# Routing on the unnormalised residual in a two-layer decoder trunk, with the residual's rows turned one tile pair at a time

## The reference

```python
x = x + y @ w_o[l]
h = rms_norm(x, ffn_norm[l])          # x / sqrt(mean(x*x) + eps) * gain
# layer 0: x = x + swiglu(h, wg, wu, wd)
# layer 1:
logits = (h @ router)                 # 256 x 8
topv, topi = top_k(logits, 2)
gates = softmax(topv)
# every expert e computes swiglu(rows of h that chose e) and adds gate * result to those rows of x
```

## Time and profile before

| | us |
|---|---|
| three runs | 1672.48, 1673.81, 1678.3; median 1673.81 |
| the profiled execution, its own time | 1672.51 |
| its span in the trace | 1670.7 |
| layer 0: mixers, dense part (to the last down product) | 0 to 467 |
| layer 1: mixers (to the last output product) | 476 to 671 |
| layer 1: norm and routing, to the first expert matmul | 671 to 702.5 |
| eight experts | 702.5 to 1661 |
| busy: TensorE, VectorE, ScalarE, GpSimd | 97%, 73%, 62%, 4% |

### The profile page before, as it was taken

How to read it: one execution, slowest core, us unless ns; L and a number is a source line. 1 busy time by engine, 2 the same in 40 slices (tenths; PEclk the granted TensorE clock), 3 DMA queues, 4 the chain that set the end, 5 groups by cost and what they waited for, 6 DMA issues and landing times.

```text
span 1670.7 us, 28450 instructions
## 1 busy us (share of the span) xinstructions
PE 1614.5 (97%) x10924; PEld 1397.2 (84%) x10924; DVE 1212.5 (73%) x1378; ACT 1034.5 (62%) x1286; POOL 60.5 (4%) x70
## 2 busy tenths in 40 slices
PE   7998989999999999799999999999999999999997
PEld 6887889999987878788888888888888888888885
DVE  1365454545424654489999999999999999999996
ACT  2334344444423343378888888888887887888885
POOL 0004000000000040000000000000000000000000
PEclk9999989999989999799999999999999999999999
DMA  6502165555414202599999999999999999999994
GB/s 202 179 17 104 55 224 178 186 192 177 159 56 152 101 4 75 183 355 376 341 392 393 352 394 394 349 395 390 350 395 388 356 393 373 366 395 362 386 385 144
DMA packets 192359, 445.59 MB, mean 267 GB/s; under 512 B 9088, under 2 KB 11664, under 8 KB 192144
## 3 DMA queue, kind: packets, MB, share of 16 engines
q1 hardware_dynamic: 187040, 433.49, 70.8%
q0 software_dynamic: 2160, 7.87, 2.1%
q10 hardware_dynamic: 3072, 3.01, 0.5%
HBM read 438.04 MB, written 6.29 MB: 266 GB/s over the span
## 4 chain that ended last, share of the span: by engine, by line
PE 95%; DVE 2%; ACT 1%; issue 1%; DMA 0%; POOL 0%; SPq 0%; ACTq 0%; DVEq 0%; POOLq 0%
PE bank L692 24%; PE bank L694 24%; PE bank L693 24%; PE bank L675 16%; PE bank L788 3%; PE bank L1234 1%; PE bank L700 1%; DMA arena<-in_consts 0%; ACT acts_hi L1297 0%; PE bank L1037 0%; DVE acts_lo L2066 0%; PE bank L1173 0%; PE bank L795 0%; DVE w_lo L1828 0%; DVE w_lo L1837 0%
## 5 line engine op out<-in xcount | busy, mean ns | idle before, releaser
L1297 ACT ACTIVATE w_hi<-ring 128x1024 fp32r<-128x1024 f32 x772 | 815.4, 1060 | 293.2 <-PE bank L694 292.5
L1837 DVE TENSOR_TENSOR w_lo<-ring,w_hi 128x1024 fp32r<-128x1024 f32 x672 | 813.0, 1224 | 67.5 <-ACT w_hi L1297 19.6
L692 PE MATMUL bank<-w_hi,acts_hi 128*128 128x512 f32 x1344 | 528.4, 393 | 7.1 <-DVE acts_lo L2066 5.7
L694 PE MATMUL bank<-w_hi,acts_lo 128*128 128x512 f32 x1344 | 523.7, 390 | 0.0
L693 PE MATMUL bank<-w_lo,acts_hi 128*128 128x512 f32 x1344 | 523.4, 389 | 0.0
L692 PEld LDWEIGHTS bank<-w_hi,acts_hi 128*128 128x128 f32 x1344 | 252.4, 188 | 59.9 <-issue 5.9
L694 PEld LDWEIGHTS bank<-w_hi,acts_lo 128*128 128x128 f32 x1344 | 252.2, 188 | 53.0
L693 PEld LDWEIGHTS bank<-w_lo,acts_hi 128*128 128x128 f32 x1344 | 252.5, 188 | 50.9
L1828 DVE TENSOR_TENSOR w_lo<-ring,w_hi 128x1024 fp32r<-128x1024 f32 x84 | 102.7, 1225 | 118.8 <-ACT w_hi L1297 118.8
L692 PE MATMUL bank<-acts_hi,w_hi 128*128 128x256 f32 x608 | 174.8, 287 | 1.6 <-DVE acts_lo L1646 1.6
L693 PE MATMUL bank<-acts_lo,w_hi 128*128 128x256 f32 x608 | 173.5, 285 | 0.0
(11 more groups left out here) (202 smaller groups left out, 1216.8 us busy)
## 6 DMA issues: line engine op xcount, KB each, us to landing
ring<-in_moe_wg SPq DMA_DIRECT2D x112, 1024.0 KB, 7.0
ring<-in_moe_wu SPq DMA_DIRECT2D x112, 1024.0 KB, 7.2
ring<-in_moe_wd SPq DMA_DIRECT2D x112, 1024.0 KB, 7.0
ring<-in_w_in SPq DMA_DIRECT2D x24, 1024.0 KB, 6.4
ring<-in_dense_wg SPq DMA_DIRECT2D x14, 1024.0 KB, 5.2
ring<-in_dense_wu SPq DMA_DIRECT2D x14, 1024.0 KB, 5.1
ring<-in_dense_wd SPq DMA_DIRECT2D x14, 1024.0 KB, 4.8
ring<-in_w_o SPq DMA_DIRECT2D x8, 1024.0 KB, 7.4
```

The lines of the kernel that those rows point to most:

```text
L692: pe.matmul(out_, a_hi, b_hi, start=first, stop=False, **kw)
L694: return pe.matmul(out_, a_lo, b_hi, start=False, stop=final, **kw)
L1297: return act.activation(o, i, ACT.Copy, **kw)
L1837: TT(w_lo[:, q, :], raw, w_hi[:, q, :].bitcast(F32), ALU.subtract).then_inc(lo_ready, 1)
```

## The change

- **Splits one pair earlier, both layers.** Pieces 0 and 1 of block g are split after pair 0 and pieces 2 and 3 after pair 1, on ScalarE and VectorE.
- **Router on the residual.** At the start of layer 1 VectorE multiplies `router_w` by the norm's gain (`router_set`). `turn_rows(i)` on TensorE turns pair i of `xT` as soon as it is added and multiplies `xT` with the router weights: nothing for pair 0, tiles 0 to 3 with pair 1, then two tiles each with pairs 2 and 3. In layer 1 `spread_rms`, the 8 scalings of `hT` and the turning of `hT` are gone. The square sums, root and reciprocal stay; the reciprocal scales the difference of the two best logits and, later, the rows.
- **Rows.** ScalarE keeps the turned `xT` (`keep_rows`), half 0 before the root and half 1 after it. VectorE makes `h_tok` as `x_tok` * reciprocal * gain in two halves (`normal_rows`), the gain read from a new input of 128 equal rows (512 KB, one DMA on ScalarE's queue, issued once the mixers are done).
- **First one-hot alone.** VectorE makes expert 0's one-hot (`hot_first`, 256 columns) straight from the counts; the ranks come after it, and the one-hot of all experts, the gates and the token numbers after the split of the gathered rows (`place_tokens`).
- **Writes of the rows.** `h_rows` and `out` are written by ScalarE's queue after the split of the gathered rows.
- `x_tok` and `h_tok` lie elsewhere, so that they can be written while the mixers' tensors are in use.

```diff
@@ -1045,6 +1053,23 @@
+            def turn_rows(i):
+                pe.wait_ge(wo_added, 4 * (L - 1) + i + 1)
+                for k in (2 * i, 2 * i + 1):
+                    for b in range(2):
+                        last = pe.transpose(bank[ROWS_BANKS[k // 4][b]][:, k % 4 * P:(k % 4 + 1) * P],
+                                            xT[:, k, b * P:(b + 1) * P], ident)
+                if i % 2:
+                    last.then_inc(pe_turned, 1)
+                pe.wait_ge(router_set, 1)
+                for k in ((), range(4), (4, 5), (6, 7))[i]:
+                    for b in range(2):
+                        last = pe.matmul(bank[1][:, b * NE:(b + 1) * NE], xT[:, k, b * P:(b + 1) * P], router_w[:, k, :],
+                                         start=k == b == 0, stop=k == KT - 1, skip_group_check=True)
+                if i == 3:
+                    last.then_inc(logit_done, 1)
@@ -1110,10 +1135,14 @@
                     if j:
                         sum_squares(2 * l + 1, 2 * j - 2)
                         sum_squares(2 * l + 1, 2 * j - 1)
+                        if l:
+                            turn_rows(j - 1)
+                if l:
+                    turn_rows(3)
                 sum_squares(2 * l + 1, KT - 2)
                 sum_squares(2 * l + 1, KT - 1)
-                spread_rms(2 * l + 1)
                 if l == 0:
+                    spread_rms(1)
@@ -1157,30 +1186,13 @@
-            for b in range(2):
-                for k in range(KT):
...
-            for f in range(8):
...
-                last.then_inc(pe_turned, 1)
@@ -1264,9 +1278,10 @@
-                pe.wait_ge(oh_ready, p + 1)
-                if p == 0:
-                    pe.wait_ge(act_turned, 4)
+                if p:
+                    pe.wait_ge(oh_ready, p + 1)
+                else:
+                    pe.wait_ge(hot_ready, 1)
                 gather(0, first)
@@ -1319,14 +1334,22 @@ (ScalarE)
-                    if between and i in (1, 2):
-                        between(range(2 * i - 2, 2 * i))
+                    if between and i < 2:
+                        between(range(2 * i, 2 * i + 2))
+                if then_keep:
+                    then_keep()
@@ -1940,15 +1968,15 @@ (VectorE)
-                    if j in (1, 2):
-                        pieces = range(2 * j - 2, 2 * j)
+                    if j < 2:
+                        pieces = range(2 * j, 2 * j + 2)
@@ -2010,17 +2038,34 @@ (VectorE)
             TT(sel, first, second, ALU.add).then_inc(route_sel, 1)
-            TT(e2, top2, top1, ALU.subtract).then_inc(route_act, 1)
+            then(TT(e2, top2, top1, ALU.subtract))
+            dve.wait_ge(rt_ready, 4)
+            then(dve.reciprocal(rms, rms))
+            TT(e2, e2, rms, ALU.mult).then_inc(route_act, 1)
+
+            def normal_rows(hf):
+                dve.wait_ge(act_turned, 2 * hf + 2)
+                hs = slice(hf * CW, (hf + 1) * CW)
+                for b in range(2):
+                    last = STT(h_tok[:, b, hs], x_tok[:, b, hs], rms[:, b:b + 1], gain_rows[:, hs], ALU.mult, ALU.mult)
+                last.then_inc(ht_ready, 1)
+
+            dve.wait_ge(gain_in, 16)
+            normal_rows(0)
             dve.wait_ge(rank_done, 1)
+            then(STT(rank_first, per(bank[6][:, 0:16])[:, :, 0], 1.0, per(sel)[:, :, 0], ALU.add, ALU.mult))
+            STT(hot_first, spread(const("iota"), 2), 1.0, stretch(rank_first, P), ALU.add,
+                ALU.is_equal).then_inc(hot_ready, 1)
+            normal_rows(1)
@@ -2090,9 +2134,14 @@ (VectorE, place_tokens is the old head of moe_pass)
                 first = p * NE
-                gathered(first)
                 if p:
+                    then(TS(rank, rank, -float(P), None, ALU.add))
+                    place_tokens()
+                    gathered(first)
                     split("g", 0, first)
+                else:
+                    gathered(first)
+                    place_tokens()
                 split("u", 0, first)
```

More of the change, by code:

```diff
@@ L120, in decoder_trunk @@
 def decoder_trunk(nc, x, consts, masks, params, lora, vres_v2, w_in, vres_w, w_o, dense_wg, dense_wu, dense_wd,
-                  router, moe_wg, moe_wu, moe_wd, h_rows, out):
+                  router, gains, moe_wg, moe_wu, moe_wd, h_rows, out):
     with ExitStack() as ctx:
@@ L235, in decoder_trunk @@
         sil_b = [moe.take(CW) for _ in range(2)]
+        hot_first = moe.take(2 * P).rearrange("p (b s) -> p b s", b=2)
+        moe.take(max(0, 22 * T - moe.at))
+        x_tok = moe.take(2 * D).rearrange("p (b d) -> p b d", b=2)
+        h_tok = moe.take(2 * D).rearrange("p (b d) -> p b d", b=2)
+        gain_rows = spare[:, 0:D]
         dense = Region(arena[:, phase:ARENA], ARENA - phase)
@@ L1157, in _ @@
                     norm(2)
-            for b in range(2):
-                for k in range(KT):
[L1162 to L1166, removed]
-            for f in range(8):
[L1169 to L1174, removed]
-                last.then_inc(pe_turned, 1)
             sel = small[:, 0:16]
             pe.wait_ge(route_sel, 1)
[L1179 to L1183, removed]
+            mm(bank[6][:, 0:8], const("tri"), sel[:, 0:8])
+            mm(bank[6][:, 8:16], const("tri"), sel[:, 8:16], True, False)
+            mm(bank[6][:, 8:16], ones, sel[:, 0:8], False, True)
+            mm(bank[6][:, 16:24], ones, sel[:, 0:8], True, False)
+            mm(bank[6][:, 16:24], ones, sel[:, 8:16], False, True).then_inc(rank_done, 1)
             def moe_pass(p):
@@ L1320, in split_in, with keep_rows, norm @@
                     copy(w_hi[:, q, :], ring[:, slot_of[n], q % 2 * PIECE:(q % 2 + 1) * PIECE]).then_inc(hi_ready, 1)
-            def norm(n, ready, between=None):
+            def keep_rows(hf):
+                act.wait_ge(pe_turned, hf + 1)
+                for b in range(2):
+                    copy(x_tok[:, b, 512 * hf:512 * (hf + 1)], bank[ROWS_BANKS[hf][b]][:, :]).then_inc(act_turned, 1)
+            def norm(n, ready, between=None, then_keep=None):
                 done, base, tiles = ready
@@ L1513, in _ @@
                 recurrence(l)
-                norm(2 * l + 1, (wo_added, 4 * l, 2), lambda pieces: split("g", 0, 0, pieces) if l else dense_split("g", 0, pieces))
+                if l:
+                    act.wait_ge(y_out, L)
+                    act.dma_start(gain_rows, gains).then_inc(gain_in, 16)
+                norm(2 * l + 1, (wo_added, 4 * l, 2), lambda pieces: split("g", 0, 0, pieces) if l else dense_split("g", 0, pieces),
+                     (lambda: keep_rows(0)) if l else None)
                 if l == 0:
@@ L1847, in _ @@
                     h_low_part(2 * l, k)
+                if l:
+                    gain0 = N_PARAM * l + PARAM_COLS["ffn_norm"][0]
+                    TT(router_w, router_w, stretch(prm[:, gain0:gain0 + KT], NE), ALU.mult).then_inc(router_set, 1)
                 head_factor(2 * l, 4, 1.0 / HD, NORM_EPS, (ALU.mult, ALU.add))
@@ L1949, in _ @@
                 dve.wait_ge(wo_added, 4 * l + 4)
-                norm(2 * l + 1, l, "ffn_norm")
                 if l == 0:
+                    norm(1, 0, "ffn_norm")
                     def dense_multiply(j):
@@ L1999, in _ @@
             dve.wait_ge(logit_done, 1)
-            then(TS(logits, bank[0][:, 0:16], 1.0, None, ALU.mult))
+            then(TS(logits, bank[1][:, 0:16], 1.0, None, ALU.mult))
             def largest(value, hot):
```

66 lines of the change are left out of this document (34 added, 32 removed).

## The result

The changed kernel takes 1658.07 us (median of 4 runs, 1657.62 to 1660.04) against 1673.19 for the kernel before: ratio 0.9915, 95% interval 0.9898 to 0.9933, 15.1 us less. Timed a second time, beside the two kernels of experiment 9, it came to 1660.31 us and 0.9927 (0.9913 to 0.9941). Forecast: 1659.7. The profiled execution took 1657.62, its span 1655.8, 14.9 less than before.

The account below looks back on a forecast made before the run. TensorE was taken as the bound, at 95% of the span. Layer 0's 1.7 us plus 12.4 before the first expert matmul made 14.1 off 1672.51, 1658.4, or 1659.7 on the median's footing; range 1655 to 1667.

Parts of the forecast that it names:

- The bound: Whole kernel: TensorE is 95% of the span, so an earlier first expert matmul moves the end by as much.
- Layer 0, 1.7: Layer 0's norm: splits one pair earlier bring the first dense matmul 1.7 us forward.
- the late sums: Layer 0's norm: TensorE's sums for the pair before stand in front of the last ones, losing 0.2 us.
- TensorE's order in layer 1: Layer 1's routing: transposes and router matmuls between the products; logits done at 676.7 and no longer at 685.4.
- Selection: Layer 1, logits to gathering: counts at low clock 2.2 us, costing 0.5; gathering starts at 682.4 instead of 695.59.
- Gathering to first matmul: Layer 1, gathering's start to first expert matmul: 7.7 us, bounds 4.9 and 8.4; that matmul 12.4 us earlier.
- The covers: Work put elsewhere around routing and expert 0 stays hidden behind other work; taken to cost 0.
- point (2): Expert 0: place_tokens after the last split delays u's splits, with 3.9 us of cover before u's first piece is due.
- The clock never falls: Layer 1's routing: TensorE stays at full clock, 3.3 us more gain, 1656.4; chance 0.12.
- the low clock lasts long: Layer 1: low clock from the last wide product into the first expert, gain 8, 1666; chance 0.12.
- The gain stays hidden: Expert 0: late weights make TensorE wait for what it wins, 1669 to 1674; chance 0.05.
- slower: Expert 0: low clock carried in, costing half of each us; 1679 with 40 us of it; chance 0.03.

Follow-up runs that it names:

- experiment 9: Changed kernel with sums of squares against 128 columns of ones, 1648.64 us; the same with router, counts and slot_pairs widened too, 1646.95 us.
- run 1: Kernel before with only the splits of block g one pair earlier in both layers: 1667.86 us, ratio 0.9975.
- run 2: Changed kernel with the splits of block g back in their old place, after pairs 1 and 2, in both layers: 1660.06 us, ratio 0.9921.
- run 3: Changed kernel with all four turn_rows after layer 1's last products instead of between them: 1662.05 us, ratio 0.9938.
- Run 5: Changed kernel with the one-hot of all experts made before the gathering and expert 0 gathered from it, without its own one-hot: 1662.32 us, ratio 0.9938.
- Run 4: Changed kernel with the whole one-hot written three times in place_tokens, 4.6 us more on VectorE: 1662.71 us, ratio 0.9939.
- All wide: Changed kernel with sums of squares 128 columns wide and the columns of router, counts and slot_pairs repeated: 1646.95 us, ratio 0.9848.

## Why the prediction was right

**The bound.** Right. What was won before the first expert matmul arrived at the end: 968.23 and 968.16 us behind it.

**Layer 0, 1.7.** Right in mechanism, small in size: 1.9 in run 1 and 2.38 here. The last square came 1.91 nearer to the first add, as forecast; the late sums, priced at 0.2, cost nothing (2.63 us from the last square to the spreading, for 2.60). The other 0.5 are the clock, a term left out: it fell at 217.2, as the spreading ended (0.71 for 1.22), where in run 1 it fell at 217.4 and the spreading began at 217.96. That is luck and not the change.

**TensorE's order in layer 1.** Right: logits 15.53 behind the first add, forecast 15.3. That the logits don't hang on the splits is run 2: with add 1 at 2.5 us behind the first one for 4.7 they come at 15.5 all the same. The step priced this work at full clock. It had that in the first profile; in the second one a low stretch within the products made the logits 1.7 later (17.35 behind the first add for 15.53), and in run 3 low clock cost 3.6 us here.

**Selection.** Right: counts at low clock (2.31, taken 2.2), the two operations on the first half of the rows 1.41 (taken 1.25), hot_first 0.42 (0.4). VectorE waited 0.59 for the counts, forecast 0.5. Run 5 prices the small one-hot at 3.0.

**Gathering to first matmul.** 7.45, forecast 7.7 between bounds of 4.9 and 8.4. It was partly at low clock, as taken. That the whole stretch met its forecast within 0.2 us (28.73, 28.6) has luck in it: the second profile has 30.22, and the gathering alone took from 5.18 to 6.07 us in kernels that leave it as it is, by where the clock was low.

**The covers.** Here is the step that failed: point (2) gave place_tokens a cover of 3.9 us up to the first piece of u, though the same sentence had slot_pairs due 1.9 behind it. Run 4 shows that slot_pairs is due first: TensorE waited 2.76 us in front of it for 4.6 us of added work, so the cover is 1.9, and each us beyond it is paid in full. With 1.9 us of cover left the forecast was not touched. The gain's DMA cost nothing: ScalarE's first piece came 0.54 behind the square, as before.

**The rivals.** "The clock never falls" came about in no run, added or widened work included; "the low clock lasts long" came in part in two profiles (1.7 us each, within the products), far from the 6 us by which it would have missed the forecast. "The gain stays hidden" and "slower" had nothing for them. The page of the Trainium skill "TensorE: Matmul & The Clock Gate", section "Part 4: PE-mode transpose", has the full clock not engage for transposes. No run separates transposes from the other work, and only the row named in the prediction bears on it: the rise at 689.3 in the kernel before, with nothing but transposes since 685.2. It does not agree with the page.

**The scatter.** 1.12 us ahead of the change's first place and 0.92 between the layers were taken as unchanged, and rightly so for the change. The first goes with the clock in the first norm, whose sums took 6.99 us in one profile and 4.95 in the other; some of these 2.0 us was lost again before the first add. Between the layers the changed kernel's clock was low from 538.1 to 541.5, in layer 1's mixers, and not in the kernel before, where the same 32 records took 1.68 us less; 0.4 were won ahead of them and 0.3 behind. The kernel before and the changed one:

```profile
541.42 7.20 PE L675 MATMUL bank<-arena,ring 128*128 128x256 f32 x32
```

```profile
537.48 8.88 PE L683 MATMUL bank<-arena,ring 128*128 128x256 f32 x32
```

## What to carry to other kernels

When a chain of small steps stands between two long matmul stages, take the norm's factor out of what only needs an order, do per tile what was done at the end, and make only the piece that the next matmul needs; then ask which engine's queue holds the result, as an earlier split was worth 1.6 us alone and nothing beside the new routing. Look for long rows of matmuls of few columns: where 128 columns cost hardly more than one (here 1.05 us for 0.95), repeating them can keep TensorE's clock up; the sums of squares alone gave 11.7 us with no instruction less, while the router, the counts and slot_pairs gave nothing that was shown. And take more than one profile before a us or two is put down to an edit: the clock's low stretches move. Ask of each cover which consumer is due first.

## What was not expected of the hardware

- Single-column float32 matmuls, back to back for 5 us behind 1.50 us without work, did not hold the clock at 2.4 GHz: it fell within them (466.4 in the changed kernel) in 11 profiles of 11, and 128 columns in their place held it in 3 of 3. All wide, the mean granted clock of the span is 0.992 for 0.984.
- The clock can fall while TensorE does wide products, with no idle time before: six products in 4.53 us for 2.85 (run 5), behind sums, transposes and router matmuls.
- Wide matmuls alone did not keep it up: all wide, it still fell behind 1.95 us without work in layer 1's routing. Behind the 2.76 us of idle time put in front of slot_pairs (run 4) it was low for 6.8 us, against 3.4 and none in the two profiles of the changed kernel.
